# The final norm behind the last gated projection: token means by transposition and a sum along the row, in a two-block transformer kernel

## The chip, the cores and the metric

One core of one Trainium2 chip runs the whole kernel. The metric is the device time in microseconds. The chip's engines work side by side, each through its own stream of instructions, and meet only at semaphores: TensorE (PE) multiplies and transposes into the PSUM memory, VectorE (DVE) and ScalarE (ACT) do the work on elements and empty PSUM, GpSimd (POOL) does small work here, SyncE (SP) issues the weight transfers.

## The reference, cut to what matters

512 tokens of width 1024 go through a first block of two layers (half FFN, mixer, half FFN, gated projection "ple"), a final norm, and a second block of two layers (hybrid mixer with attention and SSD, FFN with modulation). All is float32. The place of the change is between the blocks:

```python
def rmsnorm(x, g):
    y = x * lax.rsqrt(jnp.mean(x * x, axis=-1, keepdims=True) + EPS)
    return y * g

# end of first_block, layer 1
gate = jax.nn.sigmoid(rmsnorm(x, ple_norm[1]) @ ple_gate[1])
x = x + gate * (p[1] @ ple_proj[1])
x = rmsnorm(x, final_norm)                 # the final norm
# second_block, layer 0
h = rmsnorm_2(x, norm1_w[0]) * (1.0 + sc1) + sh1
proj = h @ w_in[0]
```

## The kernel before, in words

The residual x is kept with the 1024 features on partitions, as eight tiles of 128 features by 512 tokens. A matmul in float32 quality is made of three fp32r passes (high and low parts, `three`, L143). TensorE runs without pause through weights that SyncE loads in chunks, ScalarE and VectorE split into `wh` and `wl` (three buffers of each), and TensorE uses. Each engine's stream is written out by hand, stage by stage (`STAGES`); the stages around the change are ("ple", 1), ("final",), ("mix2", 0).

**A norm.** ScalarE squares each tile of x (`sq`, two buffers), and VectorE adds the squares over the eight tiles in `acc`. What is left is a sum over 128 partitions for each token, which goes to TensorE. There are two forms of `token_means` (L607):
- For the stages in `DEFERRED` all eight squares are in `acc`. TensorE transposes the four 128x128 parts of `acc` (tokens come to the partitions), and VectorE sums along each row into `tk`, 128x4 (`token_roots`, L2284).
- For the others `acc` holds seven tiles' squares, and the eighth stays in `sq[1]`. `means` (L593) multiplies the parts of `acc` and `sq[1]`, as stationary operands, by a column of ones (each 1/1024): one moving column each, accumulated in one bank. VectorE only copies the 128x4 result into `tk`.

GpSimd raises `tk` to the power -1/2 (`roots`, L3330, `power`, L3316) into `rtok`. `along` (L601) transposes its four columns, each broadcast to 128, so that each partition gets the root of every token: the bank called ("al", s).

**The final norm.** It is folded with the norm behind it. Two roots are needed: `r2` from the bank "tm2" (squares weighted with the gains `f2`), for the two norms together, and `rtok` from "tm", for x itself. The first is spread as ("al2", final), and VectorE's `modulated` (L2249) reads that bank in all eight of its steps, which form the input tiles h of mix2: for each tile t a product T with the root, ScalarE's high part `hh` (ScalarE's `modulated`, L1417, for tiles 2q-2 and 2q-1 behind quarter q-1), and VectorE's low part `hl`. Only the last step's end says that the bank is empty:

```python
for t in range(8):
    if t > 3:
        dve.wait_ge(lo_part, (s, "h", t - 4))
    o = dve.stt(bufs[t % 4][:, :], x[:, t, :], G[:, t:t + 1], r, MUL, MUL)
    o.then_inc(*((left(key), key) if key and t == 7 else (worked, (s, "m", t))))
```

Between the steps VectorE splits weights (behind t = 2 and t = 5), and behind t = 1 it takes the result of "tm" (`token_roots`, called from `entered`, L2269). The second root's spread form, ("al", final), is read by ScalarE's copy into R at the end of the stage, and x itself is rescaled later in mix2.

**Order on TensorE.** `entered` (L619) makes mix2's token-major product T (424 columns) in four quarters of the weights; each quarter has four blocks, one for each group of 128 tokens, of six matmuls. It holds four banks for T and one for the shift's row, whose matmul (row, through `one` and `ada`) stands behind the last block. Between blocks `final` (L787) puts the norm's operations: "tm2" behind block 2 of quarter 0, the spreading "al2" behind block 0 of quarter 1, `token_means` ("tm") behind block 2 of quarter 1, the spreading "al" behind block 0 of quarter 3. Behind the row comes the first product of mix2, xb 0 (`mix2`, L1005).

**PSUM banks.** There are eight. `take` (L471) goes round them, leaves out those held, and has TensorE wait until the last user of the chosen bank is done with it:

```python
while self.turn % 8 in self.held:
    self.turn += 1
b = self.turn % 8
self.turn += 1
if b in self.kept:
    self.pe.wait_ge(*self.kept[b])
```

Of the kernel before, what the change touches and what calls it, by code (L numbers as in the profile page):

```python
# [12 lines left out]
MUL, ADD, SUB, MAX, MIN = ALU.mult, ALU.add, ALU.subtract, ALU.max, ALU.min  # L13

D, S, NF, FT, EPS = 1024, 512, 2816, 22, 1e-6
# [158 lines left out]
def build(nc, I, out):  # L174
    with ExitStack() as ctx:
# [5 lines left out]
        def sb(name, shape, dt=F32, alias=None):  # L181
            n = 4 * int(np.prod(shape[1:]))
            o = off[0] if alias is None else alias
            if alias is None:
                off[0] += n + (-n) % 32
            return place(name, shape, dt, o), o
# [15 lines left out]
        ident = identr[:, :].bitcast(F32)  # L202
# [6 lines left out]
        sq = [sb(f"sq{i}", [128, S])[0] for i in range(2)]  # L209
        acc, _ = sb("acc", [128, S])  # L210
# [23 lines left out]
        tk = small[:, 68:72]  # L234
        t8 = [small[:, 72 + 8 * i:80 + 8 * i] for i in range(6)]
# [4 lines left out]
        tok4 = "p (b n) -> p b n"  # L240
        angle = ar[:, 41, 16:80].rearrange(tok4, b=4)

        def signal(name):
            return Signal(ctx.enter_context(nc.semaphore(name)))
# [7 lines left out]
        formed = signal("pe_formed")  # L252
        hi_split, lo_split, ada_summed = signal("hi_split"), signal("lo_split"), signal("ada_summed")
        emptied = [Emptied(ctx.enter_context(nc.semaphore(f"emptied{i}"))) for i in range(8)]
        hi_part, squared, curved = signal("hi_part"), signal("squared"), signal("curved")
        lo_part, x_new, summed, worked = signal("lo_part"), signal("x_new"), signal("summed"), signal("worked")
# [188 lines left out]
        def arrived(t):  # L445

            return (curved, ("xin", t)) if t % 2 else (x_new, (None, t))
# [42 lines left out]
        def ps(key):  # L490
            return psum[bank_of.get(key, 0)]

        def left(key):

            return emptied[bank_of.get(key, 0)]

        def left_of(key):
            return (left(key), key)
# [3 lines left out]
        def pe_program(e):  # L502
            pe = Tensor(e)
            banks = Banks(pe)
# [88 lines left out]
            def means(key, src, last=None):  # L593
                b = banks.take(key)
                n = len(src) - 1
                for k in range(4):
                    for i, a in enumerate(src):
                        done = pe.mm(b[:, k:k + 1], a[:, 128 * k:128 * k + 128], last if i and last is not None else ones[:, 0:1], i == 0, i == n)
                done.then_inc(formed, key)
# [7 lines left out]
            def token_means(s):  # L607
                if s[0] in DEFERRED:
                    b = banks.take(("tm", s))
                    pe.wait_ge(summed, (s, 7))  # L610
                    for k in range(4):
                        done = pe.tr(b[:, 128 * k:128 * k + 128], acc[:, 128 * k:128 * k + 128], ident[:, :])
                    done.then_inc(formed, ("tm", s))
                    return
                pe.wait_ge(summed, (s, 6))
                pe.wait_ge(squared, (s, 7))
                means(("tm", s), (acc, sq[1]))
# [28 lines left out]
            def opened(s, names):  # L646

                gs = [G_of[(s, *n)] for n in names]
                bs = []
                for g, n in zip(gs, names):  # L650
                    step(g)
                    begun.add(g)
                    bs.append(banks.take((s, *n), True, freed(s, n)))
                for k in range(8):
                    operand((s, "h0"), k)
                    for a in range(2):
                        hi, lo = weights(gs[a])
                        done = pe.three(bs[a][:, :], hi[:, k, :], lo[:, k, :], hh[:, k, :], hl[:, k, :], k == 0, k == 7)
                        if k == 7:
                            done.then_inc(used, gs[a])  # L660
                        if k == 2 and a == 0:
                            pe.wait_ge(pooled, ("rtok", s))
                            along(("al", s), rtok)
                    if k < 7:
                        done.then_inc(formed, (s, "h0", k))
                    if k == 0:
                        token_means(s)
                    if k == 3:
                        b = banks.take((s, "c"))
                        pe.wait_ge(worked, (s, "shift"))  # L670
                        pe.tr(b[:, 0:128], adab[:, 0:128], ident[:, :])
                        pe.tr(b[:, 128:256], adab[:, 128:256], ident[:, :]).then_inc(formed, (s, "c"))

            def enter(s):
# [3 lines left out]
                if s[0] in DEFERRED:  # L678
                    if s[0] == "ple":
                        praw = ar[:, 24:26, :].rearrange("p a n -> p (a n)").rearrange("p (b c) -> p b c", b=4)  # L680
                        pe.wait_ge(misc_in, (s, "in"))
                        for c in range(2):
                            b = banks.take((s, "pt", c), freed=(lo_part, (s, "p", c)))
                            for j in range(4):
                                done = pe.tr(b[:, 128 * j:128 * j + 128], praw[:, j, 128 * c:128 * c + 128], ident[:, :])
                            done.then_inc(formed, (s, "pt", c))
                    begin(s, names[:2], hh, hl, (s, "h"))
                    if s == STAGES[0]:
                        next(con)
                        product(s, names[2], hh, hl, (s, "h"), True)  # L690
                        token_means(s)
                        product(s, ("w3", 1), hh, hl, (s, "h"), True)
                        begun.add(G_of[(s, "w3", 1)])
                    else:
                        token_means(s)
                        product(s, names[2], hh, hl, (s, "h"), True)
                    begun.add(G_of[(s, *names[2])])
                    pe.wait_ge(pooled, ("rtok", s))
                    along(("al", s), rtok)
                    return  # L700
# [609 lines left out]
            for k in range(4):  # L1310
                pe.wait_ge(x_in[k], "all")
                for t, b in enumerate(bs):
                    done = pe.tr(b[:, 128 * k:128 * k + 128], xs_in[:, k, 128 * t:128 * t + 128], ident[:, :])
                    if k == 3:
                        done.then_inc(formed, ("xin", t))
            b = banks.take("vt0")
# [3 lines left out]
            b = banks.take("awake", freed=arrived(1))  # L1320
# [790 lines left out]
        def dve_program(e):  # L2111
            dve = Vector(e)
# [171 lines left out]
            def token_roots(s):  # L2284
                dve.wait_ge(formed, ("tm", s))
                if s[0] in DEFERRED:
                    dve.rsum(tk, ps(("tm", s))[:, :].rearrange(tok4, b=4)).then_inc(left(("tm", s)), ("tm", s))
                else:
                    dve.copy(tk, ps(("tm", s))[:, 0:4]).then_inc(left(("tm", s)), ("tm", s))

            def enter(s):
# [26 lines left out]
                if s[0] == "mix2":  # L2318
                    entered(s, ("al", s), lambda: token_roots(s))
                    return  # L2320
                token_roots(s)
                begin(s, names)
                dve.wait_ge(formed, ("al", s))
# [978 lines left out]
        def pool_program(e):  # L3302
            pool = Vector(e)
# [12 lines left out]
            def power(dst, src, w, key):  # L3316
                then(pool.tt(dst, src, mhalf[:, 0:w] if w == 4 else mhalf[:, 0:1].to_broadcast([128, w]), ALU.pow), key)
# [11 lines left out]

            def roots(s):  # L3330
                if s is not None:
                    pool.wait_ge(*left_of(("tm", s)))
                    power(rtok, tk, 4, ("rtok", s))

            def inputs(s):
# [9 lines left out]
            def ple(s, nxt):  # L3345
                if nxt[0] != "final":
                    roots(nxt)

            def final(s, nxt):
                pool.wait_ge(*left_of(("tm2", s)))  # L3350
                power(r2, r2, 4, ("r2", s))
                roots(s)
# [165 lines left out]
```

## Time and profile before

| | us |
|---|---|
| Median of 3 runs | 3163.15 (3161.61 to 3163.49) |
| The profiled execution, its own time | 3160.51 |
| Its span in the profile | 3158.7 |
| TensorE busy | 3149.1 (x14696) |
| TensorE weight load busy | 2600.0 |
| VectorE busy | 1863.4 (x2674) |
| ScalarE busy | 1167.9 (x1642) |
| GpSimd busy | 155.2 (x170) |
| Mean granted TensorE clock | 0.999 of full speed |

Times inside the profile count from the span's start. Matmuls overlap, so the time that one costs in a full stream is the distance to the next start and not its own duration. A bracket behind a row gives the idle time of that engine before the row, and the engine, tile and line that ended it. A granted clock of 1.00 is 2.4 GHz, of 0.50 is 1.2 GHz. The stretch around the change runs from about 1993 to 2023 us.

### The profile page before, as it was taken

What the parts mean: (1) busy time and instruction counts of PE and PEld (TensorE: products, weight loads), DVE (VectorE), ACT (ScalarE), POOL (GpSimd) and SP (SyncE); (2) the same over time, 40 slices, a digit from 0 to 9 for tenths busy, and PEclk for the clock granted to TensorE, in tenths of its full rate; (3) what the DMA queues carried; (4) which work ended last, traced back from release to release, by engine and by line L of the source; (5) the groups of instructions that cost most, each with busy time, mean ns of one, the idle gap of its engine ahead of it and who ended that gap; (6) DMA issues with size and microseconds to landing.
All of it is one profiled execution on the core that took longest, in us unless ns stands there. A gap on an engine that the chain in (4) does not pass through costs nothing.

```text
span 3158.7 us, 36001 instructions
## 1 busy us (share of the span) xinstructions
PE 3149.1 (100%) x14696; PEld 2600.0 (82%) x14696; DVE 1863.4 (59%) x2674; ACT 1167.9 (37%) x1642; POOL 155.2 (5%) x170
## 2 busy tenths in 40 slices
PE   9999999999999999999999999999999999999999
PEld 8888878888888888888888888887888888788887
DVE  6674367676447664457666645988433358863332
ACT  4422254322233222264322223565322235742221
POOL 2000000000000000000000000122000002300000
PEclk9999999999999999999999999999999999999999
DMA  6443322444333443332244433221332332022322
GB/s 177 147 146 124 97 84 94 134 147 147 118 113 109 147 146 114 113 94 81 90 140 144 143 113 106 84 67 41 96 103 92 100 89 81 28 93 94 107 87 74
DMA packets 334331, 339.79 MB, mean 108 GB/s; under 512 B 12502, under 2 KB 329208, under 8 KB 334168
## 3 DMA queue, kind: packets, MB, share of 16 engines
q1 hardware_dynamic: 332144, 333.80, 32.9%
q0 software_dynamic: 1792, 3.62, 0.5%
q8 instruction: 119, 1.95, 0.3%
q14 instruction: 44, 0.36, 0.0%
q10 hardware_dynamic: 232, 0.06, 0.0%
HBM read 335.36 MB, written 2.10 MB: 107 GB/s over the span
## 4 chain that ended last, share of the span: by engine, by line
PE 94%; DVE 3%; ACT 2%; issue 0%; POOL 0%; DVEq 0%; POOLq 0%
PE ps L138 93%; PE ps L141 2%; ACT ar L95 1%; DVE ar L108 1%; DVE wl L100 1%; DVE ar L100 0%; ACT wh L95 0%; ACT sp L95 0%; DVE ar L111 0%; DVE ar L123 0%; ACT L95 0%; DVE ar L105 0%; DVE small L120 0%; ACT T L95 0%; POOL small L100 0%
## 5 line engine op out<-in xcount | busy, mean ns | idle before, releaser
L100 DVE TENSOR_TENSOR wl<-raw,wh 128x1024 fp32r<-128x1024 f32 (+3 forms) x549 | 654.9, 1194 | 726.1 <-ACT wh L95 725.2
L138 PE MATMUL ps<-hh,wl 128*128 128x512 f32 x2760 | 1082.4, 392 | 0.2 <-DVE wl L100 0.2
L138 PE MATMUL ps<-hh,wh 128*128 128x512 f32 x2760 | 1075.2, 390 | 0.0
L138 PE MATMUL ps<-hl,wh 128*128 128x512 f32 x2760 | 1074.8, 389 | 0.0
L95 ACT ACTIVATE wh<-raw 128x1024 fp32r<-128x1024 f32 (+3 forms) x549 | 561.8, 1025 | 506.5 <-PE ps L138 505.4
L138 PEld LDWEIGHTS ps<-hh,wl 128*128 128x128 f32 x2760 | 518.4, 188 | 111.3 <-issue 5.0
L138 PEld LDWEIGHTS ps<-hh,wh 128*128 128x128 f32 x2760 | 518.5, 188 | 109.1
L138 PEld LDWEIGHTS ps<-hl,wh 128*128 128x128 f32 x2760 | 518.7, 188 | 105.9 <-issue 0.4
L138 PE MATMUL ps<-ul,wh 128*128 128x512 f32 x1152 | 440.5, 389 | 0.0
L138 PE MATMUL ps<-uh,wl 128*128 128x512 f32 x1056 | 411.6, 390 | 0.0
L138 PE MATMUL ps<-uh,wh 128*128 128x512 f32 x1056 | 410.9, 389 | 0.0
L138 PEld LDWEIGHTS ps<-ul,wh 128*128 128x128 f32 x1152 | 216.3, 188 | 44.7
L95 ACT ACTIVATE uh<-T 128x512 fp32r<-128x512 f32 x132 | 83.4, 632 | 443.5 <-DVE T L100 443.5
L138 PEld LDWEIGHTS ps<-uh,wh 128*128 128x128 f32 x1056 | 198.2, 188 | 41.4
L138 PEld LDWEIGHTS ps<-uh,wl 128*128 128x128 f32 x1056 | 198.2, 188 | 40.8
L95 ACT ACTIVATE T<-T 128x512 f32<-128x512 f32 (+1 forms) x92 | 56.0, 614 | 351.1 <-DVE T L100 351.1
L108 DVE SCALAR_TENSOR_TENSOR ada<-raw,small,ada 128x256 f32<-128x256 f32 x336 | 162.9, 485 | 12.0
L100 DVE TENSOR_TENSOR T<-ps,R 128x512 f32<-128x512 f32 x196 | 133.5, 686 | 46.3 <-PE ps L138 37.1
L100 DVE TENSOR_TENSOR ul<-T,uh 128x512 fp32r<-128x512 f32 x132 | 91.4, 693 | 92.1 <-ACT uh L95 92.1
L100 POOL TENSOR_TENSOR small<-small 128x4 f32<-128x4 f32 (+1 forms) x23 | 36.4, 1584 | 1766.7 <-DVE small L123 998.2
L95 ACT ACTIVATE T<-ps 128x512 f32<-128x512 f32 (+1 forms) x72 | 42.8, 598 | 179.7 <-PE ps L138 164.9
L95 ACT ACTIVATE ar<-ar 128x512 f32<-128x512 f32 (+6 forms) x69 | 73.2, 1075 | 91.7 <-DVE ar L100 54.6
(252 smaller groups left out, 2672.2 us busy)
## 6 DMA issues: line engine op xcount, KB each, us to landing
raw<-in_ffn_w SPq DMA_DIRECT2D x119, 1024.0 KB, 5.3
raw<-in_w_ada SPq DMA_DIRECT2D x48, 1024.0 KB, 5.2
raw<-in_w_gate_up SPq DMA_DIRECT2D x44, 1024.0 KB, 5.1
raw<-in_m_w_in SPq DMA_DIRECT2D x26, 1024.0 KB, 5.4
raw<-in_w_down SPq DMA_DIRECT2D x16, 1024.0 KB, 4.9
raw<-in_ffn_w SPq DMA_DIRECT2D x16, 768.0 KB, 4.2
raw<-in_w_in SPq DMA_DIRECT2D x12, 1024.0 KB, 5.3
raw<-in_m_w_out SPq DMA_DIRECT2D x8, 1024.0 KB, 4.9
```

What stands on the lines that cost most here:

```text
L95: return self.issue(lambda e: e.activation(out, in_, func, **kw))
L100: return self.issue(lambda e: e.tensor_tensor(out, a, b, op))
L108: return self.issue(lambda e: e.scalar_tensor_tensor(out=out, in0=a, scalar=s, in1=b, op0=op0, op1=op1))
L138: return self.issue(lambda e: e.matmul(out, l, r, start=start, stop=stop, skip_group_check=True))
L141: return self.issue(lambda e: e.transpose(out, in_, ident))
```

## The change

For the stage "final" alone, the means are made as in the other stages: TensorE transposes the four parts of `acc` into one bank, "ta", and the four parts of `sq[1]` into another, "tm". VectorE sums each bank along its rows (into `part`, a free corner of `small`, and into `tk`), adds the two and multiplies by 1/1024. GpSimd waits for the last of these. Everything stands at the same places in the engines' streams.

```diff
@@ TensorE, token_means
+                if s[0] == "final":
+                    for key, a in (("ta", acc), ("tm", sq[1])):
+                        b = banks.take((key, s))
+                        pe.wait_ge(*((summed, (s, 6)) if key == "ta" else (squared, (s, 7))))
+                        for k in range(4):
+                            done = pe.tr(b[:, 128 * k:128 * k + 128], a[:, 128 * k:128 * k + 128], ident[:, :])
+                        done.then_inc(formed, (key, s))
+                    return
                 pe.wait_ge(summed, (s, 6))
                 pe.wait_ge(squared, (s, 7))
                 means(("tm", s), (acc, sq[1]))
@@ VectorE, token_roots
                 dve.wait_ge(formed, ("tm", s))
                 if s[0] in DEFERRED:
                     dve.rsum(tk, ps(("tm", s))[:, :].rearrange(tok4, b=4)).then_inc(left(("tm", s)), ("tm", s))
+                elif s[0] == "final":
+                    part = t8[4][:, 4:8]
+                    dve.rsum(part, ps(("ta", s))[:, :].rearrange(tok4, b=4)).then_inc(left(("ta", s)), ("ta", s))
+                    dve.rsum(tk, ps(("tm", s))[:, :].rearrange(tok4, b=4)).then_inc(left(("tm", s)), ("tm", s))
+                    dve.own()
+                    dve.tt(tk, tk, part, ADD).then_inc(worked, ("tk", s, "sum"))
+                    dve.own()
+                    dve.ts(tk, tk, 1 / D, MUL).then_inc(worked, ("tk", s))
                 else:
                     dve.copy(tk, ps(("tm", s))[:, 0:4]).then_inc(left(("tm", s)), ("tm", s))
@@ GpSimd, roots
-                    pool.wait_ge(*left_of(("tm", s)))
+                    pool.wait_ge(*((worked, ("tk", s)) if s[0] == "final" else left_of(("tm", s))))
```

## Rows read from the trace of the kernel before

**Rows 1.** The page: busy time, share and instructions of each engine.
```profile
PE 3149.1 (100%) x14696; PEld 2600.0 (82%) x14696; DVE 1863.4 (59%) x2674; ACT 1167.9 (37%) x1642; POOL 155.2 (5%) x170
```
**Rows 2.** The chain that ended last, 1990 to 2030: start us, us, what.
```profile
2012.99 9.84 PE ps L138 x44
...
2022.85 0.60 ACT T L95
```
**Rows 3.** Timeline of TensorE, the norm's means: start us, us, engine line op, out<-in.
```profile
2003.66 0.28 PE L138 MATMUL ps<-ones,acc 128*128 128x1 f32 x2
...
2005.37 0.44 PE L138 MATMUL ps<-wl,hh 128*128 128x424 f32 x1
```
**Rows 4.** Timeline of TensorE, "al", quarter 3's end, the row, xb 0.
```profile
2012.39 0.60 PE L141 MATMUL ps<-ident,small 128*128 128x128 f32 x4
2012.74 0.44 PE L138 MATMUL ps<-wl,hh 128*128 128x424 f32 x1
...
2016.30 0.88 PE L138 MATMUL ps<-ada,small 128*128 128x424 f32 x2
2017.06 0.50 PE L138 MATMUL ps<-hh,wl 128*128 128x512 f32 x1
```
**Rows 5.** Busy time by stretch: length, PE, PEld, DVE, ACT, POOL, clock, DMA, GB/s.
```profile
2022.64:2024.31 1.67, 1.67 (x17) 1.63 (x16) 0.92 (x3) 1.47 (x2) 0.62 (x2) 1.00 0.26 25
2024.31:2030.00 5.69, 5.69 (x28) 4.75 (x26) 5.62 (x9) 5.62 (x8) 0.00 (x0) 1.00 0.54 178
```
**Rows 6.** Timeline of VectorE, from the roots' copy to the last tiles.
```profile
2006.00 0.15 DVE L111 COPY small<-ps 128x4 f32<-128x4 f32 x1
2006.08 0.74 DVE L108 SCALAR_TENSOR_TENSOR T<-x,G,ps 128x512 f32<-128x512 f32 x1
...
2007.95 1.23 DVE L100 TENSOR_TENSOR wl<-raw,wh 128x1024 fp32r<-128x1024 f32 x1 [0.48 <-ACT wh L95]
...
2013.14 0.75 DVE L108 SCALAR_TENSOR_TENSOR hl<-T,mod,hh 128x512 fp32r<-128x512 f32 x1 [0.66 <-ACT hh L95]
...
2016.26 0.74 DVE L108 SCALAR_TENSOR_TENSOR T<-x,G,ps 128x512 f32<-128x512 f32 x1
2017.31 1.41 DVE L108 SCALAR_TENSOR_TENSOR hl<-T,mod,hh 128x512 fp32r<-128x512 f32 x2 [0.31 <-ACT hh L95]
```
**Rows 7.** Timeline of ScalarE in the same stretch.
```profile
2011.43 1.06 ACT L95 ACTIVATE wh<-raw 128x1024 fp32r<-128x1024 f32 x1 [0.83 <-PE ps L138]
2012.40 1.32 ACT L95 ACTIVATE hh<-T,mod 128x512 fp32r<-128x512 f32 x2
2016.56 1.34 ACT L95 ACTIVATE hh<-T,mod 128x512 fp32r<-128x512 f32 x2 [2.84 <-PE ps L138]
```
**Rows 8.** Timeline of VectorE, a row sum and two dependent small operations elsewhere.
```profile
1949.53 0.69 DVE L123 TENSOR_REDUCE small<-ps 128x4 f32<-128x512 f32 x1 [4.41 <-PE ps L141]
1950.14 2.35 DVE L100 TENSOR_TENSOR wl<-raw,wh 128x1024 fp32r<-128x1024 f32 x2
1952.41 0.16 DVE L108 SCALAR_TENSOR_TENSOR G<-mod,VT 128x8 f32<-128x8 f32 x1
1952.60 0.17 DVE L100 TENSOR_TENSOR G<-G,VT 128x8 f32<-128x8 f32 x1
```
**Rows 9.** Timeline of GpSimd, the root of "tm".
```profile
2006.30 1.01 POOL L100 TENSOR_TENSOR small<-small 128x4 f32<-128x4 f32 x1 [5.85 <-DVE small L111]
```
**Rows 10.** Timeline of TensorE near 172, then busy time by stretch (as rows 5).
```profile
168.85 1.94 PE L138 MATMUL ps<-VT,ar 8*128 8x1 f32 x16
...
172.70 0.63 PE L138 MATMUL ps<-hl,wh 128*128 128x512 f32 x1
173.13 0.63 PE L138 MATMUL ps<-hh,wh 128*128 128x512 f32 x1
...
172.10:175.50 3.40, 3.40 (x10) 2.65 (x9) 3.10 (x12) 0.00 (x0) 0.00 (x0) 0.50 0.59 180
...
3158.70:3161.00 2.30, 0.00 (x0) 0.00 (x0) 0.00 (x0) 0.00 (x0) 0.00 (x0) 0.57 0.00 0
```

## The prediction

> **What bounds the kernel now.** I read the page's busy times first. TensorE is busy 3149.1 of the 3158.7 us [rows 1], so a change counts by what it does to TensorE's order of work. The chain that ended last says where that can be softened. At the edited spot it runs through TensorE alone up to 2022.82, the end of the next stage's first product (xb 0), and from there through ScalarE, which copies that product [rows 2]. What delays TensorE before 2022.8 therefore delays everything behind it.
>
> The timelines of TensorE, VectorE and ScalarE around 2003 to 2018 us come next. In this stretch TensorE makes the token-major product T in four quarters (0 to 3) of four blocks (one per group of 128 tokens), and the norms' small operations stand between blocks. The norm that is changed stands behind block 2 of quarter 1. Its sixteen one-column matmul passes (two for each fp32 one) begin at 2003.66, and the next block begins at 2005.37 [rows 3]: 1.71 us on TensorE. The four transpositions that spread its root ("al") start at 2012.39, behind block 0 of quarter 3, and the next block starts at 2012.74 without any idle time [rows 4]. The rest of quarter 3, the shift's row and then xb 0 (from 2017.06) follow without a gap.
>
> **The change on TensorE.** Sixteen passes go and eight 128x128 transpositions come. Four such take 0.35 us from start to next start [rows 4], and the sixteen in the first window of [rows 5] take 1.67 us, 0.10 each. Eight cost 0.7 to 0.85; I take 0.75, as they are nearest to the row of four. TensorE gains 1.71 - 0.75 = 1.0 us and reaches "al" at 2011.4.
>
> By the Trainium skill, "TensorE: Matmul & The Clock Gate", Part 4: PE-mode transpose, one transposition lasts about 275 ns in a kernel and does not count as busy for the clock. The duration shown for one agrees, but the spacing in the trace does not: by an estimate from the Trainium skill's figure the eight would cost 2.2 us, and TensorE would lose 0.5 instead of gaining 1.0.
>
> **The bank.** This decides. Besides the squares' bank "tm" the new code takes another, "ta". At this point five banks are held (four for T, one for the row), so the norms go round the other three. Call them A, B, C. Before: tm2 takes A, al2 takes B, tm takes C, al takes A, which VectorE had emptied long ago by its copy of tm2. After: tm2 A, al2 B, ta C, tm A, al B. So "al" now needs the bank of "al2", and that is emptied only by VectorE's last modulated tile (t = 7 in modulated, L2249), since all eight read the spread root there. The wait is issued by take, in TensorE's own stream, ahead of "al". Behind it wait blocks 1 to 3 of quarter 3, the row matmul and xb 0. ScalarE's tiles 6 and 7 wait for the end of quarter 3 in turn [rows 7], and VectorE's low parts wait for those [rows 6]. There is no circle, as VectorE's tile 7 needs only quarter 2's end.
>
> **When VectorE is done with al2.** Before, the scaled tile 7 starts at 2016.26 and takes 0.74: 2017.0 [rows 6]. TensorE's next use of that bank was xb 0 at 2017.06, so it cost nothing. In the changed kernel:
> - The roots' copy, 0.08 to the next start [rows 6], becomes two reductions over 128x512, an addition and a scaling. A reduction from PSUM takes 0.69, with the next start 0.61 behind it; two small dependent operations start 0.19 apart [rows 8]. So 0.61 + 0.72 (the second one waited for) + 0.19 + 0.09 = 1.6 us, which is 1.5 more.
> - From 2006.08 to 2016.26 VectorE idles 0.48 and 0.66 us, both times for ScalarE [rows 6], which itself waited for TensorE to release weights (the second time at 2011.43, [rows 7]). TensorE now comes 1.0 us sooner and VectorE 1.5 later, so both waits go. 10.18 - 1.14 = 9.0 us from 2007.6: tile 7 starts at 2016.65 and ends at 2017.4. If one wait stayed it would be 2018.0; if the small operations were free, 2017.1.
> - GpSimd's root takes 1.01 us [rows 9] and starts some 1.5 us later. It ends near 2008.8, in time for 2011.4: nothing.
> - The squares and their running sum were ready for the old block and are read by the new one at the same place: nothing. No DMA is moved, and SP's queue is passed by nothing. One more take moves all later takes one bank on, with the same distances between them: nothing, as long as each bank still meets the user that it met eight takes ago.
>
> So TensorE stands from 2011.4 to 2017.4, 6.0 us. "Al" starts at 2017.4 instead of 2012.39: **+5.0 us** at the same clock. The gain of 1.0 lies wholly inside the wait. Ends: +4.7 and +5.6. I see no cover that gives this back: xb 0 ends as much later, and ScalarE stands at it.
>
> **The clock.** In this trace the granted clock fell to 0.50, which is 1.2 GHz, from 172.1 to 175.5 us [rows 10], shortly behind a group of one-column passes of 1.9 us in an otherwise full stream. Matmuls stood 0.43 us apart in it, and eight of them cost 0.2 us extra each, 1.6 us. It also reads 0.57 right behind the end, after TensorE had stopped about 3 us before [rows 10]. A stand of 6.0 us is longer than either, so I expect TensorE to resume at 1.2 GHz in T's quarter 3 and the row, all on the path. The one fall that the trace shows lasted 3.4 us; half of such a stretch is lost: **+1.7 us**. Ends: 0 (no fall) and 3.4 (twice as long).
>
> **Sum.** 5.0 + 1.7 = +6.7 us. The profiled execution took 3160.5 us (span 3158.7, 1.8 around it), so its like comes to 3167.2. The median of the runs, 3163.15, lies 2.6 above that execution: **3169.8 us**, 0.21% slower. A measurement of this kernel can tell about 0.2%, 6.3 us, from no change, so the forecast sits at that mark.
>
> **Rivals.**
> 1. The wait comes and the clock holds: +5.0, 3168.2 us, which is within 0.2%. For it: the trace has few falls, and one group of one-column passes at this very place (1.71 us) made none. Against it: a stand is not a thin stream, and 6 us is long. 10%.
> 2. Not slower: "al" finds its bank empty. It decides at 2011.4: if VectorE's tile 7 were done by then, or if the two took different banks from those I counted, only TensorE's gain of 1.0 is left: 3162.2 us, no measurable change. Against it stands tile 7 at 2016.26 even before [rows 6], with low parts and weight splits ahead of it in order. 7%.
> 3. The clock falls behind the transpositions themselves, with no wait: -1.0 + 1.7 = +0.7, 3163.9 us. Against it: the clock read 1.00 in sixteen back-to-back transpositions and for 5.7 us behind them [rows 5]. 3%. The Trainium skill's sentence on transpositions and the clock, in the same section, is the rule for this one; those rows do not bear it out.
> 4. The wait is longer than I make it, because VectorE and ScalarE keep a mutual wait of the old chain (+0.6) and the slow clock lasts twice as long: 5.6 + 3.4 = +9.0, 3172.2 us. 7%.
>
> The forecast has the remaining 73%: the wait at one of its ends or between (4.7 to 5.6) and one fall that costs half to one and a half times 1.7 us, so +5.6 to +8.2.
>
> **How the numbers follow.** The range goes from rival 1 less 0.7 us of scatter, 3167.5, to 3171.8, short of rival 4's full price; it leaves out rivals 2 and 3 and about half of 4, and some scatter. Slower by over 0.2% starts at 3169.5: three quarters of the forecast's 73%, less a few points for scatter, and rival 4 give 0.59. Within 0.2%: the rest of the forecast, rival 1 and most of rivals 2 and 3, 0.38. Faster by over 0.2% would need 6.3 us where only 1.0 is on offer: 0.03.
>
> **What would show it.** In the changed profile: TensorE's waits get an entry of about 6 us for "VectorE T L108", ahead of four transpositions of the root; the new eight transpositions take about 0.75 us at 2003.7; VectorE's roots take 1.6 us; tile 7 still ends near 2017.4; xb 0 starts near 2022 or later; the granted clock reads 0.5 for some 3.4 us from 2017.4 on. If TensorE is not idle ahead of "al", the bank count is wrong and the forecast with it. If it is idle and the clock stays at 1.00, rival 1 holds. If the idle time is right but the end moves by under 4 us, something behind xb 0 had slack that I did not see.

## The result: 0.2% slower, by a bank that is still being read

| | before | after |
|---|---|---|
| Median of 17 runs, us | 3163.01 (3158.26 to 3164.72) | 3168.73 (3166.81 to 3171.38) |
| Ratio of the times, 95% interval | | 1.002 [1.0013, 1.0026] |
| Span of the profiled execution, us | 3158.7 | 3166.8 |
| TensorE instructions | 14696 | 14688 |
| VectorE instructions | 2674 | 2677 |

3169.8 us had been forecast, 6.7 over the 3163.15 us known then; the medians now lie 5.7 apart, and the interval reaches from 4.1 to 8.2. The slowdown itself is clear of no change; which side of 0.2% it lies on is not, as the ratio stands on that mark (the medians are 0.18% apart).

TensorE's waits in the changed kernel (engine, what it did, who it waited for; us in total, times, longest). The first entry is new:
```profile
PE ps L141 <- DVE T L108: 5.7, 1, 5.7
PE ps L138 <- POOL small L129: 3.4, 1, 3.4
PE ps L141 <- ACT ar L95: 1.2, 4, 0.5
```
TensorE's timeline of the changed kernel has the eight transpositions, the wait ahead of "al", the row and xb 0:
```profile
2003.35 0.60 PE L141 MATMUL ps<-ident,acc 128*128 128x128 f32 x4
2003.78 0.60 PE L141 MATMUL ps<-ident,sq 128*128 128x128 f32 x4
2004.14 0.44 PE L138 MATMUL ps<-wl,hh 128*128 128x424 f32 x1
...
2017.05 1.09 PE L141 MATMUL ps<-ident,small 128*128 128x128 f32 x4 [5.72 <-DVE T L108]
2017.79 0.70 PE L138 MATMUL ps<-wl,hh 128*128 128x424 f32 x1
...
2023.12 0.88 PE L138 MATMUL ps<-ada,small 128*128 128x424 f32 x2
2023.51 0.72 PE L138 MATMUL ps<-hh,wl 128*128 128x512 f32 x1
```
VectorE's timeline shows the new roots and the tile that frees the bank:
```profile
2005.69 1.28 DVE L123 TENSOR_REDUCE small<-ps 128x4 f32<-128x512 f32 x2
2007.01 0.16 DVE L100 TENSOR_TENSOR small<-small 128x4 f32<-128x4 f32 x1
2007.21 0.17 DVE L104 TENSOR_SCALAR small<-small 128x4 f32<-128x4 f32 x1
2007.29 0.74 DVE L108 SCALAR_TENSOR_TENSOR T<-x,G,ps 128x512 f32<-128x512 f32 x1
...
2016.16 0.75 DVE L108 SCALAR_TENSOR_TENSOR T<-x,G,ps 128x512 f32<-128x512 f32 x1
2024.14 1.41 DVE L108 SCALAR_TENSOR_TENSOR hl<-T,mod,hh 128x512 fp32r<-128x512 f32 x2 [7.24 <-ACT hh L95]
```
ScalarE stands behind TensorE in turn, and GpSimd's root is in time:
```profile
2023.39 1.34 ACT L95 ACTIVATE hh<-T,mod 128x512 fp32r<-128x512 f32 x2 [9.50 <-PE ps L138]
```
```profile
2007.52 1.01 POOL L100 TENSOR_TENSOR small<-small 128x4 f32<-128x4 f32 x1 [7.38 <-DVE small L104]
```
The busy time by stretch (length; PE, PEld, DVE, ACT, POOL; clock; DMA share; GB/s) of the idle time, the blocks behind it, and xb 0's start:
```profile
2011.30:2017.05 5.75, 0.03 (x2) 0.03 (x1) 5.60 (x8) 2.22 (x3) 0.00 (x0) 0.81 0.15 23
2017.05:2021.60 4.55, 4.55 (x15) 4.32 (x16) 0.00 (x0) 0.00 (x0) 0.00 (x0) 0.50 0.58 201
2021.60:2024.00 2.40, 2.40 (x12) 2.03 (x11) 0.00 (x0) 0.61 (x1) 0.00 (x0) 0.98 0.00 0
```

**How to read these together.** The two profiles are 0.32 us apart before the change comes to bear, so places are compared from the first pass of "tm2" on (1996.82 before, 1996.50 after). In the block of [rows 3] the transpositions take 0.79 us (2003.35 to 2004.14) instead of 1.71. In [rows 4] "al" started 15.57 us behind that pass; now it does 20.55 behind it, after 5.72 us in which TensorE did nothing. VectorE ended its tile 7 at 2016.91 (2016.16 + 0.75), and "al" started 0.14 us later. The roots took 1.60 us where [rows 6] had 0.08. The two waits of VectorE for ScalarE that [rows 6] has ahead of tile 7 are gone, and its next idle time is the 7.24 us at the end. Behind "al" the clock reads 0.50. Before the change it was at full speed there, as this row in the same form says (length; five busy times; clock 1.00; DMA share; GB/s):
```profile
2012.00:2017.00 5.00, 5.00 (x27) 4.33 (x25) 4.34 (x6) 2.16 (x4) 0.00 (x0) 1.00 0.17 24
```

The **stretch** from the first pass of "tm2" to the next stage's norm (the first one-column pass of acc in ffn2) holds all of it. It was 215.79 us before and is 222.76 now: +6.97. Its two marks, before and then in the changed kernel:
```profile
1996.82 0.28 PE L138 MATMUL ps<-ones,T 128*128 128x1 f32 x2
...
2212.61 0.35 PE L138 MATMUL ps<-ones,acc 128*128 128x1 f32 x2 [0.19 <-issue]
```
```profile
1996.50 0.28 PE L138 MATMUL ps<-ones,T 128*128 128x1 f32 x2
...
2219.26 0.35 PE L138 MATMUL ps<-ones,acc 128*128 128x1 f32 x2 [0.20 <-issue]
```
The experiments below are compared by this stretch.

### The profile page after: what moved, and what is told of

Same layout as the page of the kernel before. It is cut to its first block, busy times and chain, and to the rows that moved or that the text cites. A ratio compares the mean times of both kernels' runs of the same rounds, so it can differ in the third digit from the quotient of the medians.

```text
span 3166.8 us, 35988 instructions
## 1 busy us (share of the span) xinstructions
PE 3151.5 (100%) x14688; PEld 2603.7 (82%) x14688; DVE 1864.9 (59%) x2677; ACT 1168.0 (37%) x1642; POOL 155.3 (5%) x170
## 4 chain that ended last, share of the span: by engine, by line
PE 93%; DVE 4%; ACT 2%; issue 0%; POOL 0%; DVEq 0%; POOLq 0%
PE ps L138 92%; PE ps L141 2%; ACT ar L95 1%; DVE ar L108 1%; DVE wl L100 1%; DVE ar L100 1%; ACT wh L95 0%; DVE hl L108 0%; ACT L95 0%; ACT sp L95 0%; DVE ar L111 0%; DVE ar L123 0%; ACT T L95 0%; DVE T L108 0%; DVE ar L105 0%
```

## The experiments

All edits are a few lines in TensorE's stream. Kernels 1 to 7 were timed in 11 runs each, beside 33 runs of the kernel before (1 to 4, median 3161.71 us) or 27 (5 to 7, 3161.84); the last four are single executions with a profile.

**1. "al" in a bank that is free.** In the changed kernel:
```diff
                     if at == (3, 0):
                         pe.wait_ge(pooled, ("rtok", s))
+                        while banks.turn % 8 != bank_of[("ta", s)]:
+                            banks.turn += 1
                         along(("al", s), rtok)
+                        banks.turn = bank_of[("al2", s)]
```


> The changed kernel, but 'al' takes the bank of 'ta' (emptied early) and xb 0 the bank of 'al2', as before the change; all later banks are those of before. Theory (the wait for al2's bank ahead of 'al' is what costs): TensorE is not idle ahead of 'al' and 'al' starts about 1.0 us sooner than in the kernel before; but xb 0 now comes to al2's bank about 1.0 us sooner while VectorE's tile 7 ends 0.2 us later, so about 1.2 us of waiting appears ahead of xb 0, the granted clock stays at 1.00 around it, and xb 0 starts 0.2 us later than before: 3163.2 us, no measurable difference. Rival (the transpositions and VectorE's longer roots themselves delay the chain): TensorE still loses 5 us or more here: 3168 us or more.

Measured: 3163.75 us against 3161.71, ratio 1.0006 [0.9997, 1.0015]; stretch 216.01 us, +0.22. The idle time is gone from "al" and a short one stands ahead of xb 0:
```profile
2009.88 0.60 PE L141 MATMUL ps<-ident,small 128*128 128x128 f32 x4
...
2013.78 0.88 PE L138 MATMUL ps<-ada,small 128*128 128x424 f32 x2
2015.66 0.50 PE L138 MATMUL ps<-hh,wl 128*128 128x512 f32 x1 [1.00 <-DVE T L108]
```
The transpositions, the row sums and GpSimd's later start are all still there, and the loss is not. VectorE's tile 7 starts at 2014.87 in this profile and takes 0.74, so it ends at 2015.61, right before xb 0: the wait for the bank of al2 has moved there. The rival, that the added work itself delays the chain by 5 us, falls.

**2. xb 0 moved out of that bank as well.** As 1, but the last line is `banks.turn = bank_of[("tm", s)]`.

> As the run before it, but xb 0 takes the bank of 'tm', empty for 9 us, and all later takes lie one bank earlier with the same distances between them. Theory: no wait ahead of 'al' and none ahead of xb 0; what stays is TensorE's own gain of 0.9 us (0.79 instead of 1.71 in the block, as the changed kernel's timeline has it), so xb 0 starts 0.9 us sooner than before and the time is 3162.1 us. This would be the best of the kernels, by less than the runs scatter; the place of xb 0 in the profile has to show it. Rival (VectorE's roots are on the path): xb 0 starts later than before by up to 1.5 us.

Measured: 3160.14 us against 3161.71, ratio 0.9996 [0.9987, 1.0005]; stretch 214.74 us, -1.05. TensorE waits for nobody here:
```profile
2010.94 0.60 PE L141 MATMUL ps<-ident,small 128*128 128x128 f32 x4
...
2014.84 0.88 PE L138 MATMUL ps<-ada,small 128*128 128x424 f32 x2
2015.23 0.72 PE L138 MATMUL ps<-hh,wl 128*128 128x512 f32 x1
2015.79 0.39 PE L138 MATMUL ps<-hl,wh 128*128 128x512 f32 x1
```
0.92 of the 1.05 us are the transpositions. The rest is most likely a wait that the kernel before had and that I had called free, for the bank that VectorE gave back at 2017.00. There the second matmul of xb 0 starts 1.10 us behind the row of [rows 4], here 0.95, and in the changed kernel as well. In the kernel before:
```profile
2017.06 0.50 PE L138 MATMUL ps<-hh,wl 128*128 128x512 f32 x1
2017.40 0.39 PE L138 MATMUL ps<-hl,wh 128*128 128x512 f32 x1
```

**3. The bank alone.** The kernel before, with its one-column means:
```diff
                 pe.wait_ge(summed, (s, 6))
                 pe.wait_ge(squared, (s, 7))
+                if s[0] == "final":
+                    banks.turn += 1
                 means(("tm", s), (acc, sq[1]))
```


> The kernel before with its one-column means, in which the final stage only skips one bank ahead of 'tm', so that 'al' lands in al2's bank as after the change. No transposition, no row sum. Theory: 'al' waits for VectorE's tile 7, which ends at 2017.0, so TensorE is idle about 4.5 us (from 2012.4) and 'al' starts 4.7 us later than before; the clock falls too and costs 1.7 to 2.1 us on the path: +6.6 us, 3169.7. Rival (the added work on VectorE or TensorE is the cause): no idle time ahead of 'al', 3163 us.

Measured: 3167.14 us, ratio 1.0016 [1.0008, 1.0025]; stretch 222.81 us, +7.02, as in the changed kernel. Its waits and timeline:
```profile
PE ps L141 <- DVE T L108: 4.6, 1, 4.6
```
```profile
2006.05 0.15 DVE L111 COPY small<-ps 128x4 f32<-128x4 f32 x1
...
2016.31 0.74 DVE L108 SCALAR_TENSOR_TENSOR T<-x,G,ps 128x512 f32<-128x512 f32 x1
```
One skipped bank, with no transposition, no row sum and the old copy, makes the whole slowdown. TensorE is idle 1.1 us less than in the changed kernel because it comes 0.9 later and VectorE is done with tile 7 0.2 sooner (tile 7 starts 19.44 us behind the first pass of "tm2", 19.66 in the changed kernel). The clock falls the same way, for 6.8 us.

**4. The idle time filled.** The changed kernel with 25 matmuls whose result nobody reads:
```diff
                     if at == (3, 0):
+                        pe.wait_ge(*left_of(("ta", s)))
+                        pe.wait_ge(hi_part, (nxt, "h", 1))
+                        for _ in range(25):
+                            pe.mm(ps(("ta", s))[:, :], hh[:, 0, 0:128], hh[:, 1, :])
                         pe.wait_ge(pooled, ("rtok", s))
                         along(("al", s), rtok)
```


> The changed kernel with 25 matmuls of 128x512 (0.23 us apart, 5.7 us) ahead of 'al' in TensorE's stream, into the bank of 'ta', which nobody reads any more: the wait is filled with work whose result is not used. Theory: 'al' starts when it does in the changed kernel, 5.0 us later than before, since VectorE sets that; but the clock stays at 1.00 behind it, so the 2.1 us that the slow clock costs on the path are not lost: 3168.0 us by the one cause alone, 1 to 2 us under the changed kernel. Rival (the slow clock falls in time that the path has to spare, or the clock has nothing to do with the idle time): the same time as the changed kernel.

Measured: 3167.53 us, ratio 1.0017 [1.0008, 1.0026]; stretch 220.66 us, +4.87. "Al" starts 20.54 us behind the first pass of "tm2", as in the changed kernel (20.55), but at full clock:
```profile
2011.98 5.84 PE L138 MATMUL ps<-hh 128*128 128x512 f32 x25
2017.85 0.62 PE L141 MATMUL ps<-ident,small 128*128 128x128 f32 x4
...
2021.78 0.88 PE L138 MATMUL ps<-ada,small 128*128 128x424 f32 x2
```
```profile
2017.85:2023.00 5.15, 5.15 (x27) 4.65 (x28) 0.20 (x1) 0.96 (x2) 0.00 (x0) 1.00 0.52 179
```
So the 6.97 us are 4.9 of waiting and 2.1 of slow clock, by the stretches of one profile of this kernel and one of the changed one. The whole times do not show it: 3167.5 is not clear of the changed kernel's 3168.7, each beside its own runs of before. VectorE's tile 7 ends at 2017.71 in this profile (2016.97 + 0.74), and the row of the 25 matmuls at 2017.82 (2011.98 + 5.84): the filling hides the wait and adds at most 0.1 us to it.

**5 and 6. "al" moved nearer to the end of tile 7.** In the changed kernel `at == (3, 0)` becomes `at == (3, 2)`; in 6 the two statements stand behind the loop, thus behind the row.

> The changed kernel with 'al' (and its wait for al2's bank) two blocks later, behind block 2 of quarter 3. In the times of the kernel before: TensorE comes there at 2013.8, and VectorE's tile 7 still sets the start of 'al' at 2017.3. Theory (the cost is the distance from the place of 'al' to that end): idle 3.4 us ahead of 'al' instead of 5.7, then one block and the row; xb 0 starts 2.5 us later than before if the clock holds. Whether it falls behind an idle time of 3.4 us is open: with a fall 1 to 2 us more. 3164 to 3166.5 us. Rival (the idle time is a fixed price of taking a bank late, or of the transpositions): as the changed kernel, +7 us in this stretch.

> The changed kernel with 'al' at the last possible place, behind quarter 3 and the row, right ahead of xb 0. TensorE comes there at 2016.1 in the times of the kernel before, tile 7 ends at 2017.2. Theory: idle 1.1 us ahead of 'al', no fall of the clock, xb 0 (whose bank is now the empty one of 'ta') starts 0.6 us later than before: no measurable difference, 3162.5 us where the kernel before has 3162. ScalarE's copy of 'al' into R comes behind its tiles 6 and 7 anyway, so nothing else is late. Rival (ScalarE's R copy or VectorE's Tt, behind the later 'al', put a new wait on TensorE's path): more than 2 us over the kernel before, with the idle time behind xb 0.

Measured, 5: 3166.08 us, ratio 1.0015 [1.0006, 1.0023]; stretch 219.94 us, +4.15; idle 3.40. Measured, 6: 3162.55 us, ratio 1.0006 [0.9997, 1.0015]; stretch 216.49 us, +0.70; idle 1.53, where 1.1 had been expected. Timeline of 5, then of 6:
```profile
2017.22 0.62 PE L141 MATMUL ps<-ident,small 128*128 128x128 f32 x4 [3.40 <-DVE T L108]
2017.59 0.44 PE L138 MATMUL ps<-wl,hh 128*128 128x424 f32 x1
...
2018.52 0.56 PE L138 MATMUL ps<-wl,hh 128*128 128x424 f32 x1
```
```profile
2015.95 0.62 PE L141 MATMUL ps<-ident,small 128*128 128x128 f32 x4 [1.53 <-DVE T L108]
```
The idle time shrinks with the distance: 5.72, 3.40, 1.53 us. Of the +4.15 in 5, 2.5 had been worked out for the wait; 1.65 is left for the clock, which fell in 5 only 0.7 us after TensorE was at work again, and lasted 3.4 us. Behind 1.53 us it stayed at 1.00.

**7. Kernel 2 again.**

> The kernel with 'al' in the bank of 'ta' and xb 0 in that of 'tm', once more, for its runs: its first comparison left open whether its 1.05 us (from the first pass of 'tm2' to the next stage's norm in the profile) shows in the whole time. Theory: 0.9997 of the kernel before; the two sets together hold 22 of its runs. If the gain is only in that one profile, the stretch is as long here as before.

Measured: 3160.76 us against 3161.84, ratio 0.9996 [0.9987, 1.0004]; stretch 214.75 us, -1.04. The stretch repeats to 0.01 us. In whole runs neither comparison proves the gain alone: both intervals hold 1, though both medians lie below. The means of the two sets lie 0.9 and 1.4 us below those of the runs beside them. Put together (22 runs against 60, drawn anew many times), the gain comes to 1.1 us, between 0.5 and 1.8, which fits the stretch. This way of comparing was not fixed before the runs, so it supports the gain rather than proves it.

**8 to 11. Four more profiles,** three of the kernel before and one of the changed one, to see why the medians lie 5.7 us apart when the stretch says 7.0. A fall is a time in which the granted clock goes to 0.50.

> The kernel before, unchanged, for another profile. Question: from 'tm2' to the next stage's norm the profiles say +7.0 us for the change, the medians of whole runs +5.7. Theory: outside of the wait the granted clock falls in some executions and not in others, behind one-column passes, each time for 3.4 us and at a cost of about 1.5 us; an execution's span is 3157 us, plus the stretch's own difference, plus 1.5 for each fall elsewhere. So this profile holds 0 to 4 falls, a span of 3157 to 3163 that matches their number within 1 us, and possibly one fall behind 'tm', which would make its stretch 217.3 instead of 215.8. Rival (the scatter comes from something else, transfers say): the span does not follow the number of falls.

> As the one before it: the kernel before once more. Theory: the places of the falls are the same few (near 172, 2214 to 2224, 2580 and 2795 us, or behind 'tm' at 2005), their number differs, and the span follows it with 1.5 us for each. Rival: falls at other places, or a span off by more than 1 us.

> The third repeat of the kernel before, with the same two theories and the same numbers: span 3157 plus 1.5 us for each fall, against a span that doesn't follow them.

> The changed kernel once more. Theory: idle 5.7 us ahead of 'al' again, the same to 0.1 us, since it is set by the order of work; but the slow clock behind it lasts as long as chance has it, with 1.0 to 2.6 us lost, so the stretch from 'tm2' to the next norm is 221.8 to 223.4 us (222.8 in the first profile). Rival (the slow clock behind the idle time always costs the same): 222.8 within 0.1.

| profile | falls other than at the wait for the bank | stretch | 3157 + (stretch - 215.8) + 1.5 x falls | span |
|---|---|---|---|---|
| before, 1st | 1 | 215.79 | 3158.5 | 3158.7 |
| before, 2nd | 3 | 215.81 | 3161.5 | 3161.6 |
| before, 3rd | 0 | 215.81 | 3157.0 | 3156.6 |
| before, 4th | 2 | 215.80 | 3160.0 | 3159.9 |
| after, 1st | 2 | 222.76 | 3167.0 | 3166.8 |
| after, 2nd | 1 | 222.72 | 3165.4 | 3165.8 |
| kernel 1 | 0 | 216.01 | 3157.2 | 3157.5 |
| kernel 5 | 4 | 219.94 | 3167.1 | 3166.9 |

The span follows the number of falls, within 0.5 us in all thirteen profiles. No profile of the kernel before has one at the final norm. My guess that the slow clock behind the wait would cost something else each time is not borne out: the changed kernel's stretch repeats within 0.04 us, though in two profiles only. Why the medians are 1.3 us closer than the stretch is not settled. The interval of the ratio holds 7.0 us, and the number of falls elsewhere differs from run to run by more than 1.3 us' worth. The rest of the record points to that scatter: the means of the same runs lie 6.5 us apart, and against the later runs of the kernel before (medians 3161.71 and 3161.84) the changed kernel's 3168.73 is 7.0 and 6.9 us more.

## Why the prediction was right, step by step

- **The transpositions' gain**, 1.0 forecast: 0.92, from 0.79 us for the eight (0.75 forecast). The 275 ns of the Trainium skill ("TensorE: Matmul & The Clock Gate", Part 4: PE-mode transpose) are the duration of one transposition. The forecast was right to price it by its distance in a stream instead, 0.10 us in this trace.
- **The bank**: as counted. "Al" waited for VectorE's tile 7 and for nothing else, 5.7 us (6.0 forecast); kernel 3 shows the skipped bank as cause, and kernels 1 and 2 show that nothing else in the change costs time.
- **VectorE's chain**: the roots took 1.60 us (1.6 forecast), both waits for ScalarE went, tile 7 ended 20.4 us behind the first pass of "tm2" (20.6 forecast). "Al" started 4.98 us later; 5.0 had been forecast.
- **The gain lies inside the wait**: yes. Kernel 3, without the gain, is as slow.
- **The clock**: 1.7 us forecast, 2.0 to 2.1 measured. This is the term that was mis-sized. I took the one fall in [rows 10], 3.4 us long, as the measure. Here it lasted 6.8 us, from 2014.9 to 2021.7 in the first profile (worked out from the clocks 0.81, 0.50 and 0.98 of its three rows above), and 4.65 of those lay on TensorE's work, against the 3.4 that I had assumed. It was luck that the number came so close: the fall lasted twice as long as forecast, and it began 2.2 us before TensorE was at work again, which took back much of the difference. Kernel 4 shows that the cost disappears when TensorE is kept at work.
- **The place of xb 0**: "near 2022 or later" was 2023.5. The sum of the stretch, 6.7 forecast, is 6.97.
- **"It cost nothing"** for xb 0 in al2's bank before the change was wrong by 0.15 us (kernel 2).
- **The rivals**: 1 (the clock holds) falls with the reading of 0.50; 2 (no wait) with the 5.72 us; 3 (a fall behind the transpositions themselves) with kernels 1 and 2, where the clock reads 1.00 throughout the stretch; of 4 one half came, a slow clock twice as long, but at 2.0 to 2.1 us and not at 3.4; the longer wait did not. What speaks for rival 3 in the same section of the Trainium skill, that transpositions do not count as busy, is borne out by none of these profiles. The one fall that began near transpositions, 0.7 us behind their start in kernel 5, had 3.40 us of idle time just ahead of them.
- **The level**: 3169.8 us was added up from the median of three runs, 3163.15. That the 17 runs of the result have 3163.01 was luck in part, as the two later sets of the kernel before have 3161.71 and 3161.84.

## What to carry to other kernels

A further buffer taken from a rotation moves every later user on by one, so ask for each of them whose buffer it gets now and when that is given back. Here one bank more put four small transpositions behind the slowest reader of all, in the stream of the engine that bounds the kernel, and that cost 7 us to gain 0.9. Where a rotation mixes short-lived and long-lived users, place the long-lived one by hand or outside of it; and compare by a stretch between two marks of the profile, which repeated within 0.04 us here when whole runs scattered by 6.

## What the runs showed of the hardware that was not expected

The granted clock falls in this kernel where TensorE is busy all but 0.2 us of the 6 us before, for 3.4 us at a cost of about 1.5 us, in 0 to 4 places of an execution. Over the thirteen profiles these places are always the same: such a fall begins near 172 us, at 2213 to 2220, 2578 to 2585 or 2793 to 2801, each time 1 to 4 us behind the start of a group of one-column passes. The kernel before has six such groups of 16 passes (from 168.85, 1996.82, 2003.66, 2212.61, 2577.01 and 2790.21 in the first profile); behind the two at the final norm no profile has a fall, and what sets them apart is open. Busy time by stretch in the second and the third profile of the kernel before, around the last of these:
```profile
2785.00:2805.00 20.00, 19.81 (x92) 16.27 (x91) 13.02 (x20) 7.94 (x11) 1.85 (x1) 0.91 0.17 54
```
```profile
2785.00:2805.00 20.00, 19.73 (x97) 16.07 (x96) 14.73 (x23) 9.84 (x14) 1.85 (x1) 1.00 0.16 53
```
The same part of the program, 0.91 in one execution and 1.00 in the other. In the profiles these falls account for nearly all of the 5 us between the shortest and the longest span of the kernel before. So in whole times a gain of 1 us is hard to see. That the one-column passes cause them is only suggested by where they lie; no kernel here took them away at those places.
